# Taking out the products of constants between the output product and the first expert

## The reference

```python
mix = (sigmoid(ga) * (nsa_o @ w_pa) + sigmoid(gb) * (hg_o @ w_pb)) @ w_o
h = layernorm(DN_ALPHA * x + mix, ln1_g, ln1_b)
y = layernorm(DN_ALPHA * h + moe(h), ln2_g, ln2_b)

def moe(x):
    logits = x @ w_router + b_router            # 32 experts
    top_v, top_e = top_k(logits, 4)
    gate = softmax(top_v)
    # each token goes to its four experts:
    #   hh = x @ w_gu[e] + b_gu[e];  gt = min(hh[:, :1024], 7);  up = clip(hh[:, 1024:], -7, 7)
    #   out = ((up + 1) * gt * sigmoid(1.702 * gt)) @ w_dn[e] + b_dn[e]
    # and the four results are added up, weighted by gate
```

## Time and profile before

| | us |
|---|---|
| median of 3 runs | 1406.27 (1406.04 to 1407.30) |
| profiled execution, device time | 1410.19 |
| its span, first to last instruction | 1408.5 |
| PE busy | 1378.1 (98% of the span) |
| DVE busy | 435.9 (31%) |
| ACT busy | 296.7 (21%) |

### The profile page before, as it was taken

One profiled execution on the slowest core, in us unless ns is written; L12 is line 12 of the kernel. 1 busy time (PEld: TensorE's weight loads), 2 busy tenths in 40 slices (PEclk: granted clock), 3 DMA queues, 4 the chain that ended last, 5 costly groups with the idle time before them and its releaser, 6 DMA issues.

```text
span 1408.5 us, 20548 instructions
## 1 busy us (share of the span) xinstructions
PE 1378.1 (98%) x7829; PEld 657.5 (47%) x7829; DVE 435.9 (31%) x946; ACT 296.7 (21%) x507; POOL 93.3 (7%) x122
## 2 busy tenths in 40 slices
PE   9999999999999999999999999999999999999996
PEld 6667999766775433333333333333333333333332
DVE  0345774763335211122112211221122111221115
ACT  1125531342311211121111111111111111111111
POOL 0031400203000000000000000000000000000000
PEclk9999999999999899999999999999999999999998
DMA  8831350738895999999999999999999999999993
GB/s 293 291 100 57 109 165 21 216 109 261 212 355 207 366 369 427 427 429 425 429 427 429 429 428 430 426 430 427 431 426 430 429 427 430 426 431 427 430 427 124
DMA packets 77638, 476.70 MB, mean 338 GB/s; under 512 B 9522, under 2 KB 37490, under 8 KB 52690
## 3 DMA queue, kind: packets, MB, share of 16 engines
q1 hardware_dynamic: 73344, 464.85, 81.6%
q0 software_dynamic: 2288, 9.51, 1.9%
q10 hardware_dynamic: 1954, 1.63, 0.4%
HBM read 471.54 MB, written 8.59 MB: 341 GB/s over the span
## 4 chain that ended last, share of the span: by engine, by line
PE 85%; DMA 12%; DVE 2%; ACT 1%; issue 0%; SPq 0%
PE bank L1316 25%; PE bank L1349 13%; DMA big<-in_w_gu 12%; PE bank L1008 4%; PE bank L1280 4%; PE bank L1259 4%; PE bank L770 3%; PE bank L754 2%; PE bank L1175 2%; PE bank L825 2%; PE bank L827 2%; PE bank L833 2%; PE bank L1188 2%; PE bank L1252 2%; PE bank L1270 1%; PE bank L1338 1%
## 5 line engine op out<-in xcount | busy, mean ns | idle before, releaser
L1316 PE MATMUL bank<-big,gates 128*64 128x512 f32 x1536 | 338.6, 594 | 4.7 <-DMA big<-in_w_gu 4.4
L1316 PEld LDWEIGHTS bank<-big,gates 128*64 128x64 f32 x1536 | 107.1, 137 | 217.2 <-issue 204.2
L1349 PE MATMUL bank<-big,gates 128*64 128x512 f32 x768 | 171.4, 595 | 0.0
L2400 DVE TENSOR_SCALAR gates<-bank 128x512 f32<-128x512 f32 x32 | 22.1, 691 | 435.0 <-PE bank L1329 435.0
L1656 ACT ACTIVATE gates<-gates 128x512 f32<-128x512 f32 x32 | 20.1, 630 | 452.6 <-DVE gates L2400 452.6
L1349 PEld LDWEIGHTS bank<-big,gates 128*64 128x64 f32 x768 | 53.0, 137 | 114.1 <-issue 114.1
L1730 POOL TENSOR_TENSOR gates<-gates,nsaT 128x192 f32<-128x192 f32 x64 | 31.4, 511 | 982.3 <-PE bank L1359 861.0
L2423 DVE TENSOR_TENSOR work<-work,bank 128x512 f32<-128x512 f32 x128 | 82.0, 681 | 42.6 <-PE bank L1280 42.6
L2419 DVE TENSOR_TENSOR work<-work,bank 128x256 f32<-128x256 f32 x32 | 13.5, 421 | 202.2 <-PE bank L1283 202.2
L1280 PE MATMUL bank<-gates 64*128 64x512 f32 x260 | 73.4, 641 | 0.9 <-ACT gates L1666 0.9
L1664 ACT ACTIVATE gates<-bank 128x512 f32<-128x512 f32 x32 | 19.1, 597 | 258.4 <-PE bank L1283 258.4
(11 more groups left out here) (391 smaller groups left out, 1624.4 us busy)
## 6 DMA issues: line engine op xcount, KB each, us to landing
big<-in_w_gu SPq DMA_DIRECT2D x96, 2048.0 KB, 23.1
big<-in_w_dn SPq DMA_DIRECT2D x48, 2048.0 KB, 26.3
front_rows<-in_w_gu SPq DMA_DIRECT2D x16, 2048.0 KB, 23.8
front_cols<-in_w_gu SPq DMA_DIRECT2D x15, 2048.0 KB, 21.9
front_cols<-in_w_dn SPq DMA_DIRECT2D x8, 2048.0 KB, 26.6
front_rows<-in_w_dn SPq DMA_DIRECT2D x8, 2048.0 KB, 29.0
big<-in_w_in SPq DMA_DIRECT2D x5, 2048.0 KB, 8.1
big<-in_cache_cmp_kv SPq DMA_DIRECT2D x64, 128.0 KB, 2.6
```

Source lines behind the costliest of these rows:

```text
L1316: last = pe.matmul(psum[2 + n][half * CAP:(half + 1) * CAP, :], xe[:, k % 4, (k // 4) * CAP:(k // 4 + 1) * CAP], weights_gu(slot, k % 2, c ...
L1349: last = pe.matmul(psum[5][half * CAP:(half + 1) * CAP, :], act_T[:, k % 4, (k // 4) * CAP:(k // 4 + 1) * CAP], ring_dn[slot][:, k % 4, ha ...
```

## The change

All twelve products of constants between the output product and the first expert are taken out, and with them the helper that issues them. Nothing else is changed: the order of everything else, the semaphores and the DMAs stay as they are. The fourteen products of constants at the very start of the kernel are not touched.

```diff
@@ turn_h
                 for n in range(2):
                     i = 2 * at + n
-                    if i == 5:
-                        keep_busy(1)
                     pe.wait_ge(h_ready, i + 1)
@@
-            def keep_busy(n):
-
-                for _ in range(n):
-                    pe.matmul(psum[6][:, 0:2 * P], ident, const[:, 0:2 * P], start=True, stop=True)
-
@@
             turn_h(1)
-            keep_busy(1)
             router_product(1)
             turn_h(2)
-            keep_busy(1)
             router_product(2)
-            keep_busy(4)
 
             pe.wait_ge(select_ready, 3)
@@
             last.then_inc(place_done, 1)
-            keep_busy(3)
@@
             gather(0)
-            keep_busy(1)
             turn_rows(0)
-            keep_busy(1)
             pe.wait_ge(params_loaded, 80)
```

## The result

The changed kernel takes 1414.68 us (median of 5 executions, 1411.73 to 1415.25), the kernel before 1406.44 (5 executions, 1406.04 to 1407.30): a ratio of 1.0043, with a 95% interval of 1.0032 to 1.0053. The ratio is an estimate of its own and not the quotient of the two medians, which would be 1.0059. In a second comparison, side by side again, it was 1411.61 (8 executions, 1410.56 to 1415.35) against 1407.08, a ratio of 1.0033 (1.0022 to 1.0045). So the medians differ by 8.2 and by 4.5 us; the means of all executions, 13 of the changed kernel and 81 of the kernel before, differ by 5.4. The 13 lie in two groups: seven at 1410.6 to 1411.8 and six at 1414.4 to 1415.4. The forecast was 1410.2, with a range up to 1412.3. The first median lies above the range because three of its five executions are of the upper group; the median of all 13 is 1411.76.

A forecast was written before the change was run, and what follows sets the result against it. PE's order and its granted clock were taken to bound the kernel, shifts passing through one for one. Direct −1.34, gather +1.5 and tail +0.1 gave +0.3; 1406.27 + 3.6 (low stretch) + 0.3 = 1410.2 us, range 1404.8 to 1412.3.

The forecast's parts named there:

- (a): One constant at 450.27 to 450.87, ahead of a router product that waits for ACT's copy; covered, 0 saved.
- (b): One constant between 453.37 and 454.82, ahead of a half that waits for DVE's layer norm; covered, 0 saved.
- (c): One constant ahead of the last router product, which needs ACT's copy; between 0 and 0.2 us saved, taken as 0.
- (d): Four constants between the last router product and the place product, partly beside DVE's picking; 1.08 us saved.
- (e): Three constants between the place product and the gather, which waits for DVE's matrix; 0.26 us saved.
- tail of the place product: End of the place product ahead of the gather, falling out of full clock without the constants; +0.1 us.
- gather: Dense work after the place product, 2.94 us at full clock; clock expected back in its middle, +1.5 us.
- The price of their stretch: Half-clock stretch of the profiled execution, transposes to place product; 3.2 to 4.0 us, near 3.6, absent from the timed runs.
- (g): One constant after the turn, right ahead of the first expert, beside an ACT copy of 0.60 us; 0 saved.
- The third rival: Clock returns only within the first expert, whole gather low, +2.8 us in the expert; 1414.8 us, chance 0.12.
- The first rival: Profiling explains the gap; timed runs before already have the low stretch, change gives only +0.3; 1406.6 us, chance 0.22.
- The second: Rival: constants do nothing for the clock, only direct savings remain; 1404.9 or 1406.0 us, chance 0.15.

The follow-up runs named there:

- e2_abc: The kernel before with only the three constants of (a), (b) and (c) kept, the other nine gone: 1412.67 us, ratio 1.0046 to before.
- e3_efg: The kernel before with only three constants ahead of the gather, one after it and one after the turn kept: 1413.30 us, ratio 1.0040.
- e4_16col: The kernel before with all twelve constants in place, each 16 columns wide instead of 256: 1411.63 us, ratio 1.0033 to before.
- e10_fg: The kernel before with only two constants kept, beside ACT's copies between the gather and the first expert: 1411.84 us, ratio 1.0031.
- e6_abcd: The kernel before without the five constants between the place product and the first expert, those of (a) to (d) kept: 1408.34 us, ratio 1.0006.
- e12_fitted: The kernel before with constants refitted: (a) two and (b) two, (d) five instead of four, (e) two instead of three: 1406.21 us, ratio 0.9988.
- e1_d: The kernel before with only the four constants of (d) kept, the other eight gone: 1411.65 us, ratio 1.0033 to before.

## Why the prediction was wrong

The direction and the first half of the mechanism were right: without the constants the clock falls every time. The time was outside the range because one term was mis-sized, the return of the clock. By the prediction's own steps, each trace counted from the start of the residual add behind the last output product (449.60 before, 449.83 after):

| step | forecast | measured |
|---|---|---|
| (a), (b) | 0 | 0 |
| last half turned | 0 | −0.26 (1.12, then 0.86) |
| (c) | 0, at most 0.2 | 0 |
| (d) | −1.08 | −1.06 (place product at 14.01, then 12.69, less the 0.26) |
| (e) | −0.26 | −0.25 (gather 0.30 us behind DVE's matrix, then 0.05) |
| tail of the place product | +0.1 | +0.28 (1.75, then 2.03, from its start to DVE's reading of it) |
| gather | +1.5 | +2.64 (2.94, then 5.58) |
| turn and copies up to the expert | 0 | +0.39 |
| first expert | 0 | +2.80 (13.95, then 16.75) |
| rest of the loop and the stage before | 0 | +0.5 |
| profiled against profiled | +0.3 | +5.06 |

The direct savings came as worked out, −1.31 us against −1.34. That the sum up to the gather is also near the forecast (−1.29 against −1.24) is luck: the tail cost 0.18 more than forecast, and the last half was turned 0.26 faster because the clock happened to fall 0.4 us later behind the residual add (5.5 us, against 5.15 before), which no run ties to the change.

The step that failed is the sentence "The gather at half clock is as dense and would take 5.9, so I expect the clock back in its middle." In no trace whose clock was low at the place product and stayed so up to the gather was it back before the last 0.15 us of the gather: the gather took 5.58 us in all six (the changed kernel twice, e2_abc, e3_efg, e4_16col, e10_fg). So the term is +2.64 at the least and not +1.5. In both traces of the changed kernel the return missed the expert's start too, which cost another 2.8 in the expert and 0.4 on the way to it. These are of the upper group, six of thirteen executions. The lower group has no trace; its mean clock, 0.990 to 0.992, matches the traces of e2_abc and e4_16col (0.991), where the clock was back ahead of the expert. Of the prediction's signs, the fall (455.4) and the low clock in the gather came true; the gather of 4 to 5 us, the clock back before the first L1316 and an expert 0 to 1 us later (it was 1.74) did not. That the gather is as good as (d) for the clock was assumed, not shown by a row. What about it is not as good (a third of its time has only 32 of the 128 rows, its weight tiles have 64 columns, and a pause stands ahead of it and behind it) was not separated, so why the return is late stays open.

The other half of the sum stood. The profiled execution of before was indeed of a kind that the three timed runs were not: 18 of 81 further executions of that kernel are low ones. The price of their stretch, forecast as 3.6, is 3.8 between the traces of before and e6_abcd, and 3.0 between the two groups of executions on one chip (1406.97 and 1410.0). The first of these is counted up to the first expert; e6_abcd is without (e) to (g), but e12_fitted, which has them, reaches the expert as early (18.22 us behind the residual add, against 22.03 before). And after the change every one of 13 executions was low, as "it should fall every time" has it.

The third rival, a late return, gave 1414.8, the time of the upper group (1414.4 to 1415.4), by just this mechanism: whole gather low, and 2.8 in the expert. The argument against it, "the gather is denser than anything there", is the same error, and its chance of 0.12 rests on that. The first rival, that the gap is due to profiling, is out: executions of the kernel before reach 1410 without the profiler, the changed kernel reaches 1414.9 without it (1415.25 with it), and the traces of e6_abcd and e12_fitted are of profiled executions at 1406.90 and 1406.70. The second, that constants do nothing for the clock, is refuted by e4_16col and by the changed kernel itself, none of whose 13 executions keeps the clock. So is the rule of the Trainium skill that the prediction weighed ("TensorE: Matmul & The Clock Gate", the closing table), that the clock stays up without long gaps between bursts of products, for this kind of stage: e4_16col kept its pauses at 0.66 us or less and lost the clock for 17 us.

## What to carry to other kernels

Before taking out work that looks idle, read the clock column around it, and price the stage at both levels: a filler beside a wait costs nothing at full clock and may be what keeps the next 20 us at full speed. Fit fillers to the length of the wait at full clock, with wide products, and test groups of them: here (a) to (c) alone and (d) alone did little, both together nearly all. Where the clock is low already, fillers stand on the path at double length. And when one profiled execution differs by 0.3% from the runs, ask which of two levels it was, and compare mean clocks execution by execution before pricing anything against it.

## What the runs showed of the hardware

- The clock fell with PE 85% busy and no pause above 0.36 us (before, 449.4 to 454.7). What PE did then were transposes, a router product with 32 columns and two constants. In e4_16col PE was busy for 15.16 of 16.90 us, 5.6 of them in the gather with its 512 columns, and the clock did not come back in that stretch.
- Where the clock falls is not tied to the program alone. In two traces of the kernel before it fell 5.15 and 4.60 us after the start of the same instruction, the residual add behind the last output product. Over the twelve traces in which it fell early, of ten kernels, it was 3.7 to 5.6 us, and in those of e6_abcd and e12_fitted it never fell in this stage. The Trainium skill says ("TensorE: Matmul & The Clock Gate", Part 1) that the hardware's look at activity does not start over with the kernel, so that the point of change varies between runs. The traces of the kernel before agree, with 0.55 us between the two.
- A return is not for good: in e1_d the clock was back at 463.3 and fallen again at 466.7, with 2.23 us of PE's work between.
